# The output projection of a hybrid decoder layer: accumulating four output tiles side by side

## The reference

```python
mix = g[:, :, 0] * (ya @ w_pa) + g[:, :, 1] * (yb @ w_pb) + g[:, :, 2] * (yc @ w_pc)
x = x + mix.astype(x.dtype) @ w_o
h2 = rmsnorm(x, norm2)
x = x + jnp.square(jax.nn.relu(h2 @ w_up)) @ w_down
```

## Time and profile before

| | us |
|---|---|
| median of the runs shown | 895.38 |
| span of the profiled execution | 892.1 |
| TensorE busy, matmuls | 849.7 |
| VectorE busy | 593.9 |
| ScalarE busy | 413.2 |
| POOL busy | 250.6 |

### The profile page before, as it was taken

How to read it: one execution, slowest core, us unless ns; L and a number is a source line. 1 busy time by engine, 2 the same in 40 slices (tenths; PEclk the granted TensorE clock), 3 DMA queues, 4 the chain that set the end, 5 groups by cost and what they waited for, 6 DMA issues and landing times.

```text
span 892.1 us, 19937 instructions
## 1 busy us (share of the span) xinstructions
PE 849.7 (95%) x7048; PEld 831.1 (93%) x7048; DVE 593.9 (67%) x876; ACT 413.2 (46%) x583; POOL 250.6 (28%) x253
## 2 busy tenths in 40 slices
PE   3999899999899999999989999999998999999995
PEld 3999899999799999999989998999988999999995
DVE  7665758886777767455466675888578677655553
ACT  5432253465446666434353234343835566654430
POOL 5574610002860000011127843200077200001221
PEclk9999999999999999999999999999999999999998
DMA  7957557975666767777668476678666677777751
GB/s 239 295 183 232 204 153 237 306 248 178 223 223 222 250 226 250 246 246 258 207 176 269 164 241 188 231 209 289 228 218 211 212 237 235 259 260 259 255 192 48
DMA packets 167182, 200.80 MB, mean 225 GB/s; under 512 B 15568, under 2 KB 162320, under 8 KB 165776
## 3 DMA queue, kind: packets, MB, share of 16 engines
q1 hardware_dynamic: 166672, 198.37, 68.8%
q10 hardware_dynamic: 432, 1.43, 0.4%
HBM read 190.26 MB, written 51.89 MB: 271 GB/s over the span
## 4 chain that ended last, share of the span: by engine, by line
PE 71%; issue 12%; POOL 6%; DVE 5%; DMA 3%; SPq 1%; ACT 1%; POOLq 0%; DVEq 0%; ACTq 0%
PE main L545 22%; PE main L546 21%; PE main L547 20%; PE small L595 3%; DMA raw<-in_w_in 2%; POOL gated L1516 1%; PE small L760 1%; DVE w_lo L1027 1%; POOL mix_lo L1508 1%; POOL sq L1414 1%; POOL state_s L1478 1%; POOL state_s L1477 1%; DVE h_lo L1034 1%; POOL sq_sum L1415 1%; PE small L609 1%
## 5 line engine op out<-in xcount | busy, mean ns | idle before, releaser
L848 ACT ACTIVATE w_hi<-raw 128x1024 fp32r<-128x1024 f32 (+1 forms) x260 | 268.5, 1041 | 315.6 <-PE main L547 141.9
L1027 DVE TENSOR_TENSOR w_lo<-raw,w_hi 128x1024 fp32r<-128x1024 f32 (+1 forms) x260 | 343.1, 1321 | 100.2 <-ACT w_hi L848 91.0
L545 PE MATMUL main<-h_hi,w_hi 128*128 128x264 f32 x1312 | 381.2, 291 | 18.2 <-DVE w_lo L1027 18.0
L546 PE MATMUL main<-h_lo,w_hi 128*128 128x264 f32 x1312 | 373.5, 285 | 0.0
L547 PE MATMUL main<-h_hi,w_lo 128*128 128x264 f32 x1312 | 373.1, 284 | 0.0
L545 PEld LDWEIGHTS main<-h_hi,w_hi 128*128 128x128 f32 x1312 | 248.7, 190 | 23.5 <-issue 21.1
L546 PEld LDWEIGHTS main<-h_lo,w_hi 128*128 128x128 f32 x1312 | 249.1, 190 | 0.2
L547 PEld LDWEIGHTS main<-h_hi,w_lo 128*128 128x128 f32 x1312 | 247.7, 189 | 0.0
L545 PE MATMUL main<-a_hi,w_hi 128*128 128x264 f32 x512 | 145.3, 284 | 0.0
L546 PE MATMUL main<-a_lo,w_hi 128*128 128x264 f32 x512 | 145.0, 283 | 0.0
L547 PE MATMUL main<-a_hi,w_lo 128*128 128x264 f32 x512 | 145.0, 283 | 0.0
(11 more groups left out here) (187 smaller groups left out, 961.3 us busy)
## 6 DMA issues: line engine op xcount, KB each, us to landing
raw<-in_w_in SPq DMA_DIRECT2D x48, 1024.0 KB, 6.2
raw<-in_w_up SPq DMA_DIRECT2D x32, 1024.0 KB, 5.4
raw<-in_w_down SPq DMA_DIRECT2D x32, 1024.0 KB, 5.0
out_kvs<-in_cache SPq DMA_DIRECT2D x48, 512.0 KB
out_kvs<-in_cache SPq DMA_DIRECT2D x32, 496.0 KB
raw<-in_w_o SPq DMA_DIRECT2D x8, 1024.0 KB, 5.1
raw<-in_w_br SPq DMA_DIRECT2D x8, 768.0 KB, 4.6
gates<-q_scratch SPq DMA_DIRECT2D x4, 768.0 KB, 7.3
```

The lines of the kernel that those rows point to most:

```text
L545: pe.matmul(out[:, 0:TOK], wh, rh, start=start and k == 0, stop=False)
L546: pe.matmul(out[:, 0:TOK], wh, rl, start=False, stop=False)
L848: act.activation(w_hi[:, u % 4, 0:k, :], raw_of(u, k), ACT.Copy).then_inc(w_hi_ready, 1)
L1027: dve.tensor_tensor(w_lo[:, u % 4, 0:k, :], raw_of(u, k), w_hi[:, u % 4, 0:k, :].bitcast(F32), ALU.subtract).then_inc(w_lo_ready, 1)
```

## The change

TensorE takes outputs 0 to 3 in turn over each of the mix tiles 0 to 4, each in its own bank, and then completes them one after another over tiles 5 to 7. Outputs 4 to 7 follow as before. So that output 3 can start, VectorE makes the low part of w_o tile 3 ahead of the first evacuation instead of behind it; each later round then makes that of unit m + 4 instead of m + 3, and the last round none. ScalarE makes the high part of unit m + 4 ahead of `h_hi` of tile m, but for the last tile.

```diff
                 early = KT - 3
-                for ms, k0, nk in (((0, 1), 0, early), ((0, 1), early, KT - early), (range(2, KT), 0, KT)):
-                    for m in ms:
+                for k in range(early):
+                    pe.wait_ge(mix_lo_ready, l * KT + k + 1)
+                    for m in range(4):
                         u = U_O + m
-                        if k0 == 0:
+                        if k == 0:
                             pe.wait_ge(w_lo_ready, l * UNITS + u + 5)
                             pe.wait_ge(out_taken, l * OUTS + O_O + m + 1)
-                        per_k = (lambda k: pe.wait_ge(mix_lo_ready, l * KT + k0 + k + 1)) if m == 0 else None
-                        mm = unit(u % 4, main[(O_O + m) % 4], mix_hi, mix_lo, k0, nk, wk0=k0, start=k0 == 0,
-                                  stop=k0 + nk == KT, per_k=per_k)
-                        if k0 + nk == KT:
-                            mm.then_inc(w_used, 1)
+                        unit(u % 4, main[(O_O + m) % 4], mix_hi, mix_lo, k, 1, wk0=k, start=k == 0, stop=False)
+                for m in range(4):
+                    per_k = (lambda k: pe.wait_ge(mix_lo_ready, l * KT + early + k + 1)) if m == 0 else None
+                    unit((U_O + m) % 4, main[(O_O + m) % 4], mix_hi, mix_lo, early, KT - early, wk0=early, start=False,
+                         per_k=per_k).then_inc(w_used, 1)
+                for m in range(4, KT):
+                    u = U_O + m
+                    pe.wait_ge(w_lo_ready, l * UNITS + u + 5)
+                    pe.wait_ge(out_taken, l * OUTS + O_O + m + 1)
+                    unit(u % 4, main[(O_O + m) % 4], mix_hi, mix_lo, 0, KT).then_inc(w_used, 1)
...
                 for m in range(KT):
-                    norm_hi(l, 1, m)
+                    if m == KT - 1:
+                        norm_hi(l, 1, m)
                     split_hi(l, U_O + m + 4)
+                    if m < KT - 1:
+                        norm_hi(l, 1, m)
                 norm_std(l, 1)
...
+                split_lo(l, U_O + 3)
                 for m in range(KT):
                     u = U_O + m
                     unit_done(dve, l, u)
                     dve.tensor_tensor(x[:, m, :], main[(O_O + m) % 4][:, 0:TOK], x[:, m, :], ALU.add)\
                        .then_inc(out_taken, 1)
-                    split_lo(l, u + 3)
+                    if m < KT - 1:
+                        split_lo(l, u + 4)
                     norm_lo(l, 1, m)
```

## The result

The changed kernel takes 913.6 us (median of 910.75, 911.84, 915.35 and 918.43), where the kernel before takes 895.99 in the runs beside it: 1.0196 times as long, 95% interval 1.0161 to 1.0231, or 17.6 us more. The prediction said 912.7. In every execution whose span is on record the time is 1.7 to 1.9 us longer than its span. So the profiled execution of the kernel before, with a span of 892.1 us, took about 893.9 us: of the 3.3 us to the median only 1.8 lie outside the span, and the rest is that this execution was quicker than the median one.

What follows compares the result with a forecast made beforehand. TensorE's matmul stream, 95% busy, was taken as the bound. Stall, displaced work and tail 13.3 to 15.3 us plus clock 3.6 made 16.9 to 18.9; taken as +17.3 on 895.4: 912.7 us, range 906 to 918.5.

Steps and rivals of the forecast that it cites:

- Step 1: w_o stage: output 3 waits for the w_o tile 3 split behind the last mix tile; TensorE restarts 1.15 us later.
- Step 2: Before the restart TensorE does 9 matmuls instead of 36; the 27 displaced cost 3.3 us a layer.
- step 3: After the restart, VectorE's rounds and the w_up transfer delay the sum of squares: 13.3 to 15.3 us for both layers.
- B: Piece from output 0's evacuation to output 7's; layer 0 forecast from 249.0 to between 266.8 and 267.8.
- A: Piece from the first w_o matmul to output 0's evacuation; the forecast put that evacuation at 249.0 in layer 0.
- The piece C: From output 7's evacuation to TensorE's sum of squares; taken as unchanged at 3.08 us.
- The split that left round 7: Shortens the end of VectorE's queue by 1.1 us, but was said to gain nothing, as the squares follow the evacuation.
- Step 4: TensorE's clock falls to 1.2 GHz after the restart in both layers: 1.8 us a layer, 3.6 in all.
- Rival B: Only the stall counts, VectorE catches up in the w_o tail: +10.8 us, 906.2 us; chance 0.12.
- Rival C: Heavier w_o tail: low clock lasts twice as long, transfers take 6.4 us; about +22.5, 918 us; chance 0.12.
- Rival D: w_lo of tiles 2 and 3 ready by 233.8, TensorE fills the w_o tail: 8.1 us faster, 887.3; chance 0.03.
- "Four banks instead of two are free": Bank use in the w_o stage was said to cost nothing, since outputs 0 to 3 had four banks before, too.

Runs made afterwards that it cites:

- the run with the weights first: Changed kernel with h_lo of x tiles 0 and 1 made in VectorE's round 2 instead of rounds 0 and 1: 915.85 us, ratio 1.0216.
- The fillers: Changed kernel plus 50 unused matmuls a layer, placed where TensorE waits for the splits of w_o tiles 2 and 3: 909.59 us, ratio 1.0152.
- the run with two outputs and the weights first: Kernel before, TensorE order kept; VectorE makes h_lo of x tiles 0 to 2 behind w_o splits 3 to 5, last split last: 895.97 us, ratio 0.9998.

## Why the prediction was right

By its own steps, on intervals of the stage:

- *Step 1, the new wait.* The restart was to come 1.15 us later. It's 8.77 us after the first w_o matmul, where before the stream ran freely from 240.25 - 232.63 = 7.62 on the earlier trace rows: 1.15. The split stands at 240.46 behind `mix_lo` at 240.11, 0.35 us, as worked out.
- *Step 2, the displaced work.* Nine matmuls before the restart, as said, each group within 0.1 us of its place; the waits of 2.65 and 3.53 us were forecast as 2.7 and 4.0. The matmuls of output 2 ran on the low clock already, which made the second shorter. The step's count of what output 0 takes is right from the restart on (60), but output 0 is finished after 69 of the 192 matmuls, not after 60 as step 3 says; the sum doesn't use that figure.
- *Step 3, the tail.* B was to be 17.8 to 18.8 us (249.0 to 266.8 and 267.8) and is 17.96 and 17.94. Round 4's wait and the transfer behind it (issue to pick-up 5.56 us) are there. What this step had wrong in kind is how far the transfer can be separated from VectorE's own work, which the run with the weights first showed.

  Two further errors of the step offset each other in part. By its own figures the low part of w_o tile 5 is ready at 249.0 + 2.26 + 0.35 + 1.22 = 252.8, not at 253.6; that slip goes through to the last evacuation and makes the sum 0.8 us a layer too long. And it had VectorE go through four rounds without idling, where in round 0 VectorE waits 0.66 us for the high part of w_o tile 4, which ScalarE can't make before output 0 is done. The transfer was issued 4.5 us after the first evacuation, against 4.9 as written and 4.1 by the step's own figures. More important is what B did in the other runs. In five kernels with the changed order on VectorE and four outputs it is 17.94 to 17.96 us while A runs from 8.84 to 18.66. So the sum of squares follows the end of output 0 one for one. That's how the prediction worked it out, but it put the blame in two parts, stall and tail, where there's one: output 0 ends late, through the stall, the clock and the 60 matmuls behind the restart.
- *The piece C was taken as 3.08 us and is 2.49.* "The split that left round 7" was costed at nothing. It's worth 0.6 us a layer, as POOL's last square then runs without VectorE's split beside it; the run that moves that split alone shows it, with 0.8.
- *Step 4, the clock.* I took 1.8 us a layer. From the restart to the evacuation of output 0 it took 9.70 and 9.90 us, where 60 matmuls at 0.121 and 0.3 make 7.6: 2.1 and 2.3. The fillers gave back 1.9 and 2.3. It's the term that was too small, by 0.4 us a layer, and it makes up for part of C. One of the sightings behind it was misread: at the start of the kernel the records show no fall because they have nothing there. The trace's first record of the clock stands at 18.56 us, at 1.00, and the fast spacing begins with the matmul at 18.50. In all thirteen profiles these two lie within 0.1 us of each other, though the first record stands anywhere from 17.0 to 20.4 us. The 2.0 us read from the spacing stand.

Sum of the stage: 17.3 predicted, 16.7 in the profile; the time itself 17.6, with an interval of 14.4 to 20.7. That 912.7 and 913.6 lie so close is in part luck: the slip and C made the forecast too long, round 0 and the clock too short. What is right is the path, and that the largest terms are near. Rival B, a tail in which VectorE catches up, is out. In layer 0 TensorE starts its last w_o matmul at 266.05, and VectorE evacuates that output at 269.47, 3.1 us after it has ended. Rival C, the heavier tail, didn't come. Rival D decided where it was said to: with the split early and the outputs in turn TensorE has 0.54 us of waiting left in one tail and none in the other, but it gains 2.1 us, not 8.1, since behind it VectorE's rounds set the pace. "Four banks instead of two are free" holds.

## What to carry to other kernels

Before work is interleaved to fill a gap, look up when each operand of the first pass is ready. An engine that works in order puts the latest of them ahead of everything behind it; taken one output after another, the same work fills the gap. When a stage ends in a chain of rounds on another engine, and those rounds set the pace, its end follows the first result handed over, so the first output should be finished first. And a tail that TensorE fills pays only if the rounds behind it have room: here the third output was worth 3.8 us with a better order on VectorE and nothing that can be told without it.

## What the runs showed that I had not expected

- The clock fell in tails where TensorE never waited long: in the run with two outputs and the weights first both layers had slow matmuls, and in that of the kernel before one had. In the tails of the profiles with three or four outputs in turn it didn't fall, and no more than 2 matmuls of the stage had the slow spacing. That's about 1.5 us at stake in a tail with waits of 0.5 to 1.1 us.
- The four runs of the changed kernel lie 7.7 us apart, and go with the mean clock of the span: 0.980 at 910.75, 0.979 at 911.84, 0.977 at 915.35, 0.972 at 918.43. Of a span of 908.9 us 2.0% are 18.2 us, of 916.6 us 2.8% are 25.7: 7.5 us more, nearly the whole difference if TensorE had work in all of the low stretches. Only the run of 911.84 has a trace, and there part of the low stretch at 236 us is the stall itself, so this is an upper bound.
- POOL's square of a tile takes 0.6 us when it starts while VectorE stands idle, and 1.4 to 1.6 when VectorE is in a weight split, in all thirteen profiles.
